# Start of a fused eight-core encoder layer on Trainium2: work of the first two token groups reordered, their gate products moved to GpSimd

## The reference, cut to what matters

```python
def _layer(x, pool_hist, pos0, norm1_g, w_in, pool_w, pool_scale, gmlp_ws, gmlp_b, w_out, norm2_g, w_up, w_down):
    h = _rmsnorm(x, norm1_g)
    z = h @ w_in
    a = z[..., :POOL_WIDTH]                                       # 512 columns
    u = jax.nn.gelu(z[..., POOL_WIDTH:POOL_WIDTH + GMLP_WIDTH])   # 512
    v = jax.nn.gelu(z[..., POOL_WIDTH + GMLP_WIDTH:])             # 512
    pool_out, new_hist = _pool_mixer(a, pool_hist, pos0, pool_w, pool_scale)
    gmlp_out = _gmlp_gate(u, v, gmlp_ws, gmlp_b)
    x = x + jnp.concatenate([pool_out, gmlp_out], axis=-1) @ w_out
    f = _rmsnorm(x, norm2_g) @ w_up
    x = x + jnp.square(jax.nn.relu(f)) @ w_down
    return x, new_hist, v
```

## Time and profile before

| what | value |
|---|---|
| time, median of 3 runs | 1274.48 us (1247.42, 1274.48, 1275.45) |
| the profiled execution's own time | 1246.84 us |
| its span, slowest core (core 3) | 1245.3 us |
| spans of the 8 cores | 1242.0 to 1245.3 us |
| PE busy | 1232.7 us, 99% of the span |
| DVE busy | 504.1 us, 40% |
| ACT busy | 377.8 us, 30% |
| POOL busy | 95.2 us, 8% |
| chain of work that ended last, PE's share | 96% |

### The profile page before, as it was taken

One profiled execution on the slowest core, in us unless ns is written; L12 is line 12 of the kernel. 1 busy time (PEld: TensorE's weight loads), 2 busy tenths in 40 slices (PEclk: granted clock), 3 DMA queues, 4 the chain that ended last, 5 costly groups with the idle time before them and its releaser, 6 DMA issues.

```text
span 1245.3 us, 19363 instructions; the slowest of 8 cores (1242.0 to 1245.3 us)
## 1 busy us (share of the span) xinstructions
PE 1232.7 (99%) x6917; PEld 656.4 (53%) x6917; DVE 504.1 (40%) x931; ACT 377.8 (30%) x740; POOL 95.2 (8%) x176
## 2 busy tenths in 40 slices
PE   9899999999999999999999999999999999999998
PEld 5555545556545554554555455455545545554554
DVE  4864434444534432442444254234415433450313
ACT  6353313135312330432233043223304322420422
POOL 4110000001010000100000010000001000000000
PEclk9999999999999999999999999999999999999999
DMA  9999958449548536844853784496378439647752
GB/s 190 185 238 202 237 139 176 138 123 316 193 130 258 203 127 215 252 169 154 241 210 128 223 261 169 142 227 223 135 228 263 169 128 255 138 166 226 254 205 85
DMA packets 90544, 240.53 MB, mean 193 GB/s; under 512 B 57201, under 2 KB 57329, under 8 KB 67666
## 3 DMA queue, kind: packets, MB, share of 16 engines
q1 hardware_dynamic: 77328, 187.08, 47.2%
q0 software_dynamic: 12944, 51.88, 18.7%
q10 hardware_dynamic: 178, 0.33, 0.1%
HBM read 214.47 MB, written 34.43 MB: 200 GB/s over the span
## 4 chain that ended last, share of the span: by engine, by line
PE 96%; DVE 2%; DMA 1%; issue 0%; ACT 0%; SPq 0%; POOL 0%; DVEq 0%; ACTq 0%; POOLq 0%
PE ps L732 30%; PE ps L801 28%; PE ps L616 9%; PE ps L448 8%; PE ps L694 7%; PE ps L714 7%; PE ps L484 4%; PE ps L823 2%; DVE PQ L529 1%; DMA X<-xall 1%; PE ps L564 1%; PE ps L369 0%; DVE HB L341 0%; PE ps L594 0%; DVE DT L537 0%
## 5 line engine op out<-in xcount | busy, mean ns | idle before, releaser
L732 PE MATMUL ps<-H2T,RING 128*128 128x384 bf16 x2304 | 384.2, 326 | 0.0
L801 PE MATMUL ps<-RING,ST 128*128 128x512 bf16 x1632 | 353.7, 379 | 0.0
L732 PEld LDWEIGHTS ps<-H2T,RING 128*128 128x128 bf16 x2304 | 223.8, 98 | 147.3 <-issue 0.7
L801 PEld LDWEIGHTS ps<-RING,ST 128*128 128x128 bf16 x1632 | 159.7, 98 | 191.7
L317 ACT ACTIVATE JUNK<-X 128x1024 bf16<-128x1024 f32 (+3 forms) x103 | 106.1, 1030 | 434.0 <-DVE X L808 290.1
L736 ACT ACTIVATE ST<-ps 128x384 bf16<-128x384 f32 x288 | 140.8, 490 | 208.2 <-PE ps L732 208.1
L738 DVE TENSOR_TENSOR ST<-ST 128x384 bf16<-128x384 bf16 x288 | 96.7, 356 | 192.2 <-ACT ST L736 192.2
L808 DVE TENSOR_TENSOR X<-ps,X 128x512 f32<-128x512 f32 x48 | 33.2, 692 | 210.4 <-PE ps L801 210.4
L448 PE MATMUL ps<-HT,WAU 128*128 128x384 bf16 x640 | 106.5, 326 | 0.4 <-ACT HT L363 0.4
L448 PEld LDWEIGHTS ps<-HT,WAU 128*128 128x128 bf16 x640 | 62.2, 98 | 41.7 <-issue 1.2
L714 PE MATMUL ps<-RING,ST 128*128 128x512 bf16 x384 | 83.7, 379 | 0.0
(11 more groups left out here) (123 smaller groups left out, 714.2 us busy)
## 6 DMA issues: line engine op xcount, KB each, us to landing
RING<-scr SPq DMA_DIRECT2D x144, 1024.0 KB, 6.3
RING<-w_mlp POOLq DMA_DIRECT2D x16, 1024.0 KB, 15.1
scr<-RING SPq DMA_DIRECT2D x16, 1024.0 KB, 10.9
X<-xall POOLq DMA_DIRECT2D x27, 512.0 KB, 6.3
yall<-X POOLq DMA_DIRECT2D x27, 512.0 KB, 13.3
X<-xall SPq DMA_DIRECT2D x6, 512.0 KB, 10.4
yall<-X SPq DMA_DIRECT2D x5, 512.0 KB, 10.5
WAU<-w_au POOLq DMA_DIRECT2D x8, 256.0 KB, 11.8
```

The lines of the kernel that those rows point to most:

```text
L732: i_ = e.matmul(bank(ub)[:, 0:TOK], lhsT=RING[s][:, k, (m % 4) * 128:(m % 4 + 1) * 128], rhs=H2T[:, k, :], start=(k == 0), stop=(k == 7))
L801: i_ = e.matmul(bank(n)[:, :], lhsT=ST[:, kg * 8 + kk, n * 128:(n + 1) * 128], rhs=RING[s][:, kk, :], start=(kg == 0 and kk == 0), stop=(k ...
```

## The change

The change acts on the first two groups alone, up to their output projection, besides the number of `GT` buffers.

1. The spare products between the transposes of group 0 go from 4, 4 and 3 to 1, 2 and 2.
2. The halo's square is taken right behind the first tile's, its scaling in front of group 1's first tile, and its transposes and projection come earlier. Group 1's first tile gets its root by ACT and DVE instead of POOL.
3. Group 1's last two tiles are projected jointly, in matmuls of 256 columns. Of group 1's first tile 8 blocks are still done alone.
4. `gen_gate_mask` and `gen_foldw` move from behind the pooling of group 1 to its middle.
5. The first output half of group 0 is multiplied ahead of group 1's gate pieces, and the fold of the second half behind them.
6. The gate products of groups 0 and 1 go to POOL; `GT` has three buffers.
7. The third ring load is started ahead of group 2's X tiles.

```diff
-        GT = [sb(f"GT{j}", [128, TOK], F32) for j in range(1)]
+        GT = [sb(f"GT{j}", [128, TOK], F32) for j in range(3)]
...
-                add("dve", lambda e, g=g, gj=gj: e.tensor_tensor(out=B.MIXT[:, g, :], in0=GT[gj][:, :], in1=B.UT[:, g, :],
+                add("pool" if i < 2 else "dve", lambda e, g=g, gj=gj: e.tensor_tensor(
+                    out=B.MIXT[:, g, :], in0=GT[gj][:, :], in1=B.UT[:, g, :],
                                                                 op=ALU.mult),
...
-        def gen_WO_pe(i, squares=False, n0=0, n1=NT, kind="2"):
+        def gen_WO_pe(i, squares=False, n0=0, n1=NT, kind="2", hhs=(0, 1)):
...
-                for hh in range(2):
+                for hh in hhs:
...
-        for n in range(NT):
-            first_sq(0, n)
-            entry_root(n)
-            first_apply(0, n)
+        first_sq(0, 0)
+        entry_root(0)
+        first_apply(0, 0)
+        norm_square("1", NT, XH, [("X", 2, 0)], 16)
+        first_sq(0, 1)
...
-        gen_warm(4)
+        gen_warm(1)
         gen_N1_T(0, 1, 2)
-        gen_warm(4)
+        gen_warm(2)
         gen_N1_T(0, 2, 3, shared=True)
-        gen_warm(3)
+        gen_warm(2)
...
-        gen_WI_au(1, 0, 6, 1, 2)
...
-        gen_WI_au(1, 6, 8, 0, 2)
-        gen_PL(0, 3, 4)
-        gen_WI_au(1, 0, 8, 2, 3)
-        gen_PL(1)
+        gen_WI_au(1, 6, 8, 0, 1)
+        gen_WI_au(1, 0, 8, 1, 3)
+        gen_PL(1, 0, 2)
         gen_gate_mask()
         gen_foldw()
+        gen_PL(1, 2, 4)
         ring_load(1)
+        ring_load(2)
         gen_L(2)
...
         gen_fold(0)
         gen_WI_v(1, 2, 3)
-        gen_fold(1)
+        gen_WO_pe(0, hhs=(0,))
         for k in range(4):
             p1[k]()
+        gen_fold(1)
         for n in range(NT):
-            gen_WO_pe(0, squares=True, n0=n, n1=n + 1)
+            gen_WO_pe(0, squares=True, n0=n, n1=n + 1, hhs=(1,))
```

More of the change, by code:

```diff
@@ L858, in emit_rows, with entry_root @@
                 ev()
-        def entry_root(n):
-            add("act", lambda e: e.activation(out=RT[:, n:n + 1], in_=SS["1"][:, n:n + 1], func=AF.Sqrt, bias=EPSC[:, 0:1],
+        def entry_root(n, kind="1"):
+            add("act", lambda e: e.activation(out=RT[:, n:n + 1], in_=SS[kind][:, n:n + 1], func=AF.Sqrt, bias=EPSC[:, 0:1],
                                               scale=1.0),
-                reads=[("SSc", "1", n), "EPSC"], writes=[("RT", n)])
-            add("dve", lambda e: e.reciprocal(out=RS["1"][:, n:n + 1], in_=RT[:, n:n + 1]),
-                reads=[("RT", n)], writes=[("RS", "1", n)])
+                reads=[("SSc", kind, n), "EPSC"], writes=[("RT", n)])
+            add("dve", lambda e: e.reciprocal(out=RS[kind][:, n:n + 1], in_=RT[:, n:n + 1]),
+                reads=[("RT", n)], writes=[("RS", kind, n)])
         gen_warm(5)
@@ L881, in build_nc @@
         load_wau(7)
-        for n in range(NT):
-            first_sq(0, n)
-            entry_root(n)
-            first_apply(0, n)
+        first_sq(0, 0)
[3 more added lines that the diff above has]
+        first_sq(0, 1)
+        entry_root(1)
+        first_apply(0, 1)
+        first_sq(0, 2)
+        entry_root(2)
+        first_apply(0, 2)
         gen_N1_T(0, 0, 1)
-        gen_warm(4)
+        gen_warm(1)
         gen_N1_T(0, 1, 2)
-        gen_warm(4)
+        gen_warm(2)
         gen_N1_T(0, 2, 3, shared=True)
-        gen_warm(3)
+        gen_warm(2)
+        norm_rs("1", NT, NT + 1, 16)
+        add("dve", lambda e: e.scalar_tensor_tensor(out=HBH, in0=XH, scalar=RS["1"][0:16, NT:NT + 1], in1=G1B[0:16],
+                                                    op0=ALU.mult, op1=ALU.mult),
+            reads=[("X", 2, 0), ("RS", "1", NT)] + G1k, writes=DTall)
         first_sq(1, 0)
-        norm_rs("2", 0, 1)
+        entry_root(0, "2")
         load_wv(0)
@@ L896, in build_nc @@
         load_gate_parts()
+        load_wout(0)
         first_apply(1, 0)
@@ L899, in build_nc @@
             reads=["WSMTS"], writes=["JUNK"])
[L900 to L904, removed]
+        gen_WI_au(0, 0, 2)
+        norm_T((HBH, DTall), HT, ("HT", NT), 0, 16)
+        gen_WI_au(0, 2, 3)
         gen_N1_T(1, 0, 1, shared=True)
         gen_WI_au(0, 3, 4)
-        add("dve", lambda e: e.scalar_tensor_tensor(out=HBH, in0=XH, scalar=RS["1"][0:16, NT:NT + 1], in1=G1B[0:16],
-                                                    op0=ALU.mult, op1=ALU.mult),
-            reads=[("X", 2, 0), ("RS", "1", NT)] + G1k, writes=DTall)
+        gen_WI_halo()
         first_sq(1, 1)
@@ L916, in build_nc @@
         gen_WI_au(1, 0, 4, 0, 1)
+        gen_PL(0, 0, 1)
         gen_WI_au(0, 4, 5)
[L918 to L921, removed]
         first_sq(1, 2)
         norm_rs("2", 2, 3)
-        gen_PL(0, 0, 1)
         first_apply(1, 2)
-        gen_PL(0, 1, 3)
+        gen_PL(0, 1, 4)
+        gen_WI_au(0, 5, 6)
+        gen_WI_au(1, 4, 6, 0, 1)
+        gen_WI_au(0, 6, 7)
         gen_N1_T(1, 1, 2)
-        gen_WI_au(0, 6, 7)
-        gen_WI_au(1, 0, 6, 1, 2)
         gen_WI_au(0, 7, 8)
         gen_N1_T(1, 2, 3)
-        gen_WI_au(1, 6, 8, 0, 2)
-        gen_PL(0, 3, 4)
-        gen_WI_au(1, 0, 8, 2, 3)
-        gen_PL(1)
+        gen_WI_au(1, 6, 8, 0, 1)
+        gen_WI_au(1, 0, 8, 1, 3)
+        gen_PL(1, 0, 2)
         gen_gate_mask()
         gen_foldw()
+        gen_PL(1, 2, 4)
         ring_load(1)
+        ring_load(2)
         gen_L(2)
-        for at in range(2, 5):
-            ring_load(at)
+        ring_load(3)
+        ring_load(4)
         gen_setup_late()
```

## The result

The changed kernel takes 1255.2 us (median of 5 runs, 1253.88 to 1255.99). It stands to the kernel before as 1.0063, with a 95% interval of 1.0041 to 1.0084. That is 7.9 us slower, small but clear. The ratio leaves out executions like the two of 1274.48 and 1275.45 us that stood above; two such ones of a later session (1274.42 and 1274.50 us) show a mean granted clock of 0.973 to 0.975 on two cores and of 0.997 or more on the other six. In three later sessions the kernel before had medians of 1247.67, 1247.92 and 1247.48 us.

What follows compares the result with a forecast made beforehand. PE, busy 99% of the span, was taken as the bound. A point reached 3.45 us later, plus 1.6 for a low clock and 1.8 at the entry, gave 6.85 on 1246.84: 1253.7 us, range 1247 to 1283.

Steps and rivals of the forecast that it cites:

- against the runs shown: Step weighing the profiled execution (beside the lowest run, 1247.42) against the median of 1274.48 us; range widened to 1247 to 1283.
- low clock at the entry: Fewer spare products before PE's start at 16.93 may leave the clock low; counted as 1.8 us, between nothing and 2.
- Mask wait gone, DVE's pooling as late as before: PE's 3.2 us wait for the gate's mask goes, but group 1's pooling on DVE still ends at 50.9.
- Wait for banks: First wait: PE waits 1.6 us in all for DVE to empty the banks of the first two gate pieces.
- Wait for POOL: Second wait: PE waits 3.3 us for four gate products on POOL before the first output half, from 57.4.
- Wait for the casts: Third wait: PE waits 4.4 us before the second output half for the fold's casts, over on DVE at 68.55.
- The cost of one low clock: 1.6 us, taken from the kernel before, added once behind the third wait of 4.4 us.
- The sign that the first L617 of group 1 would start near 74 to 77 us: Sign of being right: group 1's output projection on PE starts near 74 to 77 us.
- One low clock or two: One low clock counted, behind the third wait; the 3.3 us second wait might add as much again, not counted.
- two low clocks: Rival, chance 0.2: a low clock behind the second wait as well, 1255.3 us.
- The rival that the low clock doesn't come there: Rival, chance 0.2: no low clock at the entry, as 8 spare products stay in front; 1251.9 us.

Runs made afterwards that it cites:

- fold_first: Changed kernel with the second fold moved ahead of the first output half; 1246.92 us, ratio 0.9994 to the kernel before.
- casts_act: Changed kernel with the second fold written back by ACT in place of DVE; 1250.09 us, ratio 1.0019 to the kernel before.
- Fill: Changed kernel with 14 spare products in PE's wait for POOL and 16 in its wait for the casts; 1250.75 us, ratio 1.0023.
- spares_back: Changed kernel with 4, 4 and 3 spare products again in place of 1, 2 and 2; 1254.72 us, ratio 1.0055.
- mask_only: Kernel before with only the gate's mask and the scaling of the maps moved into group 1's pooling; 1247.47 us, ratio 1.0001.
- pool_early: fold_first, plus the waiting ring load and two small loads put behind group 0's products on POOL; 1244.08 us, ratio 0.9967.
- old_tail_again: Repetition of old_tail, two of whose four runs were disturbed; 1244.53 us, ratio 0.9974 to the kernel before.
- old_tail: Changed kernel with products on DVE and the former order of fold, gate pieces and output projection; no ratio, runs of 1243.7, 1245.26, 1354.95, 1498.14 us.
- adds_first: old_tail with the bias additions of the first three gate pieces ahead of the products on DVE; 1243.56 us, ratio 0.9967.

## Why the prediction was right in its waits and wrong in its clock and its base

The forecast was 6.85 us more than the profiled execution, and 7.9 us more were measured. But the base failed. The figure of 1253.7 us stands 20.8 us under the median of 1274.48 us that was shown, and read against that median it says "faster". My step "against the runs shown" is the one that failed there: it took both levels into the range, up to 1283 us, and left open which of them the kernel before would be measured by. The runs showed the lower one: later medians of the kernel before of 1247.5 to 1247.9 us, and no run of the changed kernel above 1255.99 us. The profiled execution was the right base, and against it the forecast says slower by 0.5%.

That the sum of 6.85 us then comes so near is luck in part. The layout of the waits held: the first output half was to start at 57.4 us and did at 57.44. But the low clock behind the waits was put at 1.6 us and cost 5.75 on the slowest core, while 1.8 us stood for a low clock at the entry that did not come. The second error hides nearly half of the first.

Step by step:

- **Mask wait gone, DVE's pooling as late as before.** Right: 50.9 forecast, 50.98 in the trace.
- **Wait for banks.** Forecast 1.6 us, measured 1.3.
- **Wait for POOL.** Forecast 3.3 us, measured 3.5, with products of 0.88 us in place of 1.0 but a start at 53.67 in place of 53.2. The rule of the Trainium skill (GPSIMD Engine Reference, section on engine selection) of about half of VectorE's pace would have given 1.12 us as an estimate; the ratio here is 0.88 to 0.56, or 1.6.
- **Wait for the casts.** Forecast 4.4 us, measured 4.0, though casts and need both came later than laid out: the casts ended at 71.05 in place of 68.55. fold_first and casts_act show that it hangs on the place of the casts in DVE's list.
- **The cost of one low clock: mis-sized.** I carried over the 1.6 us of the kernel before. On the slowest core it was 2.9 us each time; over the eight cores it was 0 to 2.9 us behind the first wait and 1.7 to 2.9 us behind the second. The sign that the first L617 of group 1 would start near 74 to 77 us held on the other seven cores (73.59 to 77.02) and failed on core 4 (79.22).
- **One low clock or two: wrong.** I left the wait for POOL uncounted, and it brought the second. The rival "two low clocks" is what happened on the slowest core and on four others; cores 2, 5 and 6 had the second alone. Fill shows 5.0 us for both together, with unchanged waits. The forecast had read core 1's wait of 2.35 us as one that leaves the clock up. Core 2 of the same trace waited 2.36 us, and its eight v matmuls took 3.20 us:

```profile
51.22 1.24 PE L564 MATMUL ps<-WSMT,V 128*128 128x128 bf16 x12 [2.36 <-DVE WSMT L290]
52.25 3.20 PE L484 MATMUL ps<-WV,H2T 128*128 128x512 bf16 x8
```

  The length of a wait alone thus doesn't tell whether the clock falls.
- **Low clock at the entry, 1.8 us: wrong.** PE's first real matmuls, sixteen from 15.45 on, took 2.76 us, which is the high clock. The rival that the low clock doesn't come there, held at 0.2, is what happened. Going by the durations of transposes and spare products, the clock was up with the second transposes or the spare products behind them on seven cores, and with the third transposes on core 2. PE even started at 15.45 in place of 16.93. That gained nothing, since DVE's pooling is held by the last tile of group 1, whose square on ACT waited for its load until 27.0, and spares_back shows no difference. ACT's timeline, core 4:

```profile
27.00 1.06 ACT L317 ACTIVATE JUNK<-X 128x1024 bf16<-128x1024 f32 x1 [0.88 <-DMA X<-xall]
```

Put together up to the start of group 1's output projection, core 4 after against core 3 before: start 1.5 us earlier; waits 9.7 in place of 3.9 us (among them 0.6 for weights that now come late, and 0.4 for a transposed tile); low clock 5.75 in place of 1.6 us; some 0.4 us left over. That makes 8.9 us. In my sum the waits stood with 9.3, and the low clock with 3.4 us.

So the gain that the early mask should bring by itself was never there to take. PE came to the same DVE list a little earlier and waited for its next entry (mask_only, ratio 1.0001). The loss came from the casts behind group 1's gate (fold_first takes it all back), and from the products behind a ring load that has nothing to do with them (pool_early, another 3 us). On the slowest core each brought a low clock.

What stays open: the entry, the joint projection, the order of the loads and the `GT` buffers together are worth some 3 us (old_tail_again against mask_only), and I didn't take them apart. Why the same wait brings the low clock on one core and not on another stays open too.

## What to carry to other kernels

On engines that work in order, a wait is moved, not removed, when what stands behind it hangs on the same queue; write out the waited-for engine's new list to the end before counting a gain. Put the few instructions that the busiest engine waits for (bank releases, casts of weights) ahead of bulk work, and a DMA start that waits behind the computing that doesn't. Price each wait of TensorE of several microseconds with the slow matmuls behind it, and look at all cores: for waits of 3.5 and 4.0 us that was 0 to 2.9 us, and the slowest core, which sets the time, paid 2.9 us for each.

## What the runs showed of the hardware that I had not expected

- The low clock outlasted much of the work behind it. PE was busy without a gap from 57.44 on, and the windows of the changed kernel still read 0.50 at 62 to 63 us; the high clock came back within the next:

```profile
62.00:63.00 1.00, 1.00 (x4) 0.36 (x3) 0.00 (x0) 0.00 (x0) 0.00 (x0) 0.50 1.10 180
63.00:64.00 1.00, 1.00 (x5) 0.38 (x4) 0.00 (x0) 0.00 (x0) 0.00 (x0) 0.83 1.00 164
```

  In the kernel before, matmuls that began at 51.76 had the high clock at 55 to 56 us.
- The same wait costs different cores differently. Behind 3.5 us of waiting, the half of 24 matmuls took 5.2 us on three cores and 8.1 us on one.
- Short waits in a row can bring the low clock. In mask_only, a wait of 1.0 to 2.1 us and one of 0.95 us, with one matmul between them, brought it on six of eight cores. In old_tail and old_tail_again, 0.4 to 1.4 us and 0.76 us brought it on six of sixteen. The one bank wait that is left in adds_first (0.74 to 1.34 us) brought it on none of eight.
- A product of 128x384 with two inputs takes 0.88 us on GpSimd, 1.6 times DVE's.
